# Row products moved behind the first gate groups, and another order for the first loads of a transformer block kernel

## The reference

```
h = rmsnorm(x) * g_attn;  p = h @ w_in            # 2048 x 4944, split into latents, q, k, v, indexer
y_a = latent attention (8 heads, low-rank q and kv, rotary, chunk mask)
y_b = sparse attention (8 heads, indexer picks 64 keys per query, relative bias)
x = x + concat(y_a, y_b) @ w_o
h = rmsnorm(x) * g_ffn
# PEER, per token and per head (8 heads):
score = (h @ w_pq) . sub_keys                     # 2 x 128 scores
top 16 of each half -> 256 sums -> top 16; expert = i0 * 128 + i1;  g = softmax(top sums)
x = x + sum_k g_k * gelu(u_tab[expert_k] . h) * v_tab[expert_k]     # tables 16384 x 2048
```

## Time and profile before

| | |
|---|---|
| time, median of 3 runs | 1678.68 us (1678.19 to 1679.05) |
| the profiled execution | 1682.57 us, its span 1680.8 us |
| TensorE busy | 1653.3 us (98%), granted clock 0.998 |
| VectorE, ScalarE, POOL busy | 1019.2, 503.3, 293.3 us |
| DMA | 569.90 MB, mean 339 GB/s |
| one u product on VectorE (L1136) | 2.29 us, the next starts 2.21 after it |
| one `gate` (L1198) | 1.17 us |
| one `hots` (L1184, two instructions) | 1.21 us from start to start of the next |
| one `apply` (L1208) | 0.32 us |
| a pair of u chunks with its gate group, from 790 to 1080 us | 9.48 us |

### The profile page before, as it was taken

The page is one execution under the profiler, slowest core; times in us unless marked ns, Lnnn a source line. Parts: engine busy times, 40 slices in busy tenths (PEclk is TensorE's granted clock), DMA queues, the critical chain, the costliest instruction groups (busy, mean ns, idle before and its releaser), DMA issues.

```text
span 1680.8 us, 28829 instructions
## 1 busy us (share of the span) xinstructions
PE 1653.3 (98%) x11428; PEld 1568.1 (93%) x11428; DVE 1019.2 (61%) x1708; ACT 503.3 (30%) x1346; POOL 293.3 (17%) x252
## 2 busy tenths in 40 slices
PE   7999999999999999989999999999999999999999
PEld 5768888888999999979999999999999999999998
DVE  5426695767778999767777667663334333433343
ACT  6547567656551000134454444420000000000000
POOL 1020000000003222322212111122212212223220
PEclk9999999999999999999999999999999999999999
DMA  9764445466648999999999999999999999999996
GB/s 337 240 142 131 138 132 194 138 223 204 224 154 347 421 403 421 397 400 421 394 422 406 421 408 422 375 388 416 417 415 417 417 416 422 422 422 422 421 417 236
DMA packets 107056, 569.90 MB, mean 339 GB/s; under 512 B 11280, under 2 KB 13456, under 8 KB 48208
## 3 DMA queue, kind: packets, MB, share of 16 engines
q1 hardware_dynamic: 57056, 216.51, 34.8%
q0 software_dynamic: 31792, 220.50, 32.7%
q10 hardware_dynamic: 18144, 132.13, 19.2%
HBM read 563.04 MB, written 4.46 MB: 338 GB/s over the span
## 4 chain that ended last, share of the span: by engine, by line
PE 78%; DVE 12%; DMA 6%; ACT 1%; issue 1%; POOL 1%; SPq 0%; DVEq 0%; ACTq 0%; POOLq 0%
PE ps L1574 32%; PE ps L1519 19%; PE ps L1315 5%; PE ps L1317 5%; PE ps L1316 5%; DVE late L1136 3%; PE ps L1334 2%; PE ps L1468 2%; PE ps L1536 2%; PE ps L1470 2%; PE ps L1469 2%; DMA raw<-in_w_in 1%; DMA acts<-in_u_rows,sel 1%; DMA late<-in_u_rows,sel 1%; DVE w_lo L817 1%
## 5 line engine op out<-in xcount | busy, mean ns | idle before, releaser
L1140 DVE SCALAR_TENSOR_TENSOR acts<-late,sel,acts 128x2048 f32<-128x2048 f32 x77 | 181.1, 2351 | 246.5 <-DMA late<-in_v_tab,sel 246.1
L1519 PE MATMUL ps<-acts,raw 128*128 128x160 f32 x2048 | 289.3, 301 | 0.0
L1519 PE MATMUL ps<-acts,late 128*128 128x160 f32 x2048 | 287.9, 300 | 0.0
L1574 PE MATMUL ps<-acts,late 128*128 (+1 forms) x2048 | 284.2, 299 | 0.0
L1574 PE MATMUL ps<-acts,raw 128*128 (+1 forms) x2048 | 283.6, 300 | 0.2 <-DMA raw<-in_v_tab 0.2
L1519 PEld LDWEIGHTS ps<-acts,raw 128*128 128x128 f32 x2048 | 282.1, 191 | 0.0
L1519 PEld LDWEIGHTS ps<-acts,late 128*128 128x128 f32 x2048 | 280.5, 190 | 0.0
L1574 PEld LDWEIGHTS ps<-acts,raw 128*128 128x128 f32 x2048 | 279.9, 190 | 0.6 <-issue 0.6
L1574 PEld LDWEIGHTS ps<-acts,late 128*128 128x128 f32 x2048 | 280.1, 190 | 0.1
L817 DVE TENSOR_TENSOR w_lo<-raw,w_hi 128x512 fp32r<-128x512 f32 (+1 forms) x288 | 188.8, 682 | 134.9 <-ACT w_hi L544 132.9
L1315 PE MATMUL ps<-w_hi,hT_hi 128*128 128x512 f32 (+1 forms) x448 | 185.7, 415 | 13.5 <-DVE w_lo L817 13.2
(11 more groups left out here) (220 smaller groups left out, 1575.7 us busy)
## 6 DMA issues: line engine op xcount, KB each, us to landing
raw<-in_w_in SPq DMA_DIRECT2D x72, 512.0 KB, 3.7
raw<-in_u_tab SPq DMA_DIRECT2D x33, 1024.0 KB, 9.7
late<-in_u_tab SPq DMA_DIRECT2D x33, 1024.0 KB, 9.9
raw<-in_v_tab SPq DMA_DIRECT2D x32, 1024.0 KB, 9.3
raw<-in_v_tab ACTq DMA_DIRECT2D x32, 1024.0 KB, 9.2
late<-in_v_tab SPq DMA_DIRECT2D x32, 1024.0 KB, 9.1
late<-in_v_tab ACTq DMA_DIRECT2D x32, 1024.0 KB, 9.3
raw<-in_u_tab ACTq DMA_DIRECT2D x31, 1024.0 KB, 9.7
```

What stands on the lines that cost most here:

```text
L1140: V.scalar_tensor_tensor(acc, row[n % NROW], w_sp[:, n - N_OWN:n - N_OWN + 1], acc, ALU.mult, ALU.add).then_inc(row_used, 1)
L1519: ins = mm(ps[:, q, 0:N_DN], ring[q][:, k * P:k * P + P], hF[:, k, :], start=k == 0, stop=k == KD - 1)
L1574: ins = mm(ps[:, pair_bank(k // 2), at:at + N_DN], ring[q][:, k * P:k * P + P], acts[:, ds(i * (4 * N_DN) + q * N_DN, N_DN)], start=first ...
```

## The change

It makes these edits.
- VectorE's order at the first gate groups: `next_row(4)` ahead of the slot transposes becomes `next_row(2)`, and three more products between `hots(1)` and `apply(FIRST_G + 1)` are taken away. To make up, the loop skips a product only where c % 16 is 15, and `WEIGH_AT` moves from 120 to 122.
- The first piece of xT and the gains are issued by ScalarE; SP begins with the first unit of w_in.
- POOL waits for the first half unit on TensorE before it issues iota, rope_tab, chunk_mask and rope_gain.
- ScalarE does an activation on a one-column tile first, TensorE does five matmuls on a zeroed tile first; VectorE sets both tiles and no longer waits for its memset.

```
-                if n == 0:
-                    sp.dma_start(gains[:, :], io["gains"]).then_inc(gain_in, 16)
+                if n:
+                    sp.dma_start(xT[:, k, :], io["xT"][:, k, :]).then_inc(xT_in[n], 16)
                 load(n, n, win[:, k, 0:512])
...
             pool.dma_start(acts[0:32, A_BIAS + 512:A_BIAS + 520], io["rel_bias"]).then_inc(hot_in, 16)
+            pool.wait_ge(piece_used, 1)
             pool.dma_start(iota[:, :], io["iota"]).then_inc(mask_in, 16)
...
+            act.dma_start(xT[:, 0:2, :], io["xT"][:, 0:2, :]).then_inc(xT_in[0], 16)
+            act.dma_start(gains[:, :], io["gains"]).then_inc(gain_in, 16)
+            act.wait_ge(warm_set, 1)
+            nc.scalar.activation(table_warm, carrier, ACT.Copy)
             act.wait_ge(gain_in, 16)
...
-            link(V.memset(kpad, 0.0))
+            V.memset(carrier, 0.0).then_inc(warm_set, 1)
+            V.memset(kpad, 0.0).then_inc(warm_set, 1)
...
-        WEIGH_AT = NKEY - 8
+        WEIGH_AT = NKEY - 6
...
             V.tensor_copy(w_sp, slot[:, 2, 0:N_PICK]).then_inc(gsp_ready, 1)
-            next_row(4)
+            next_row(2)
             dve.wait_ge(slotT_mm, TT)
...
             hots(0)
             hots(1)
-            next_row(2)
             apply(FIRST_G)
-            next_row()
             apply(FIRST_G + 1)
             next_row()
             gate(0)
             hots(2)
             apply(FIRST_G + 2)
             next_row()
             gate(1)
...
-                if rows_done[0] < N_OWN and c % 8 != 7:
+                if rows_done[0] < N_OWN and c % 16 != 15:
                     next_row()
...
+            pe.wait_ge(warm_set, 2)
+            for _ in range(5):
+                mm(ps[:, 6, 0:256], kpad[:, 0, :], early[:, 1024:1280], start=True, stop=True)
             for j in range(8):
                 pe.wait_ge(hTlo_done, 2 * j + 2)
```

More of the change, by code:

```diff
@@ L247, in build_block @@
         hs_in, idx_in, gsp_in, mask_set, acc_set, turn_kept = sem("hs_in"), sem("idx_in"), sem("gsp_in"), sem("mask_set"), sem("acc_set"), sem("turn_kept")
-        lent_in, acc_sum = sem("lent_in"), sem("acc_sum")
+        lent_in, acc_sum, warm_set = sem("lent_in"), sem("acc_sum"), sem("warm_set")
         gsp_ready, a_done, w_ready, acc_in = sem("gsp_ready"), sem("a_done"), sem("w_ready"), sem("acc_in")
@@ L365, in _ @@
                 k = slice(2 * n, 2 * n + 2)
-                sp.dma_start(xT[:, k, :], io["xT"][:, k, :]).then_inc(xT_in[n], 16)
-                if n == 0:
-                    sp.dma_start(gains[:, :], io["gains"]).then_inc(gain_in, 16)
+                if n:
+                    sp.dma_start(xT[:, k, :], io["xT"][:, k, :]).then_inc(xT_in[n], 16)
                 load(n, n, win[:, k, 0:512])
```

## The result

The changed kernel takes 1670.72 us (1668.14 to 1678.65, 20 runs), the kernel before on the same chips 1679.38 us (1675.95 to 1681.89, 20 runs). The ratio is 0.995, with a 95% interval of 0.9942 to 0.9957: 7.2 to 9.7 us less, by the medians 8.7. The forecast was 1667.3, 11.4 us less; the range, 1664.3 to 1672.3, holds the result, but it lies where the rival of the late rows was put, 1670 to 1675. The profiled execution of the changed kernel took 1671.05 us with a span of 1669.3.

The account below looks back on a forecast made before the run. TensorE was taken as the bound, busy 1653.3 of 1680.8 us. Gains of 10.9 us at the first gate groups and 0.5 at the head sum to 11.4: 1678.7 - 11.4 = 1667.3 us, range 1664.3 to 1672.3 for 8 in 10.

Parts of the forecast that it names:

- the rival of the late rows: Gathers fall behind and `hots` is late; TensorE waits 3 to 8 us between 800 and 1100 us: 1670 to 1675, chance 0.15.
- the hole: TensorE's two waits at gate groups 1 and 2, 740 to 760 us, plus slow matmuls behind: 10.97 us, taken as 10.9.
- The walk: Step through VectorE, ScalarE and TensorE at the first gate groups with measured durations: both waits close, 0.7, 0.7 and 0.2 us spare.
- the differences carry over: Gains read in the profiled execution, 1682.57 us, were taken to hold for the median of the runs, 1678.68, 3.9 lower.
- the moved products cost 0: Chunks 52 to 119 carry 64 products instead of 59; cost to TensorE taken as 0, bounds 0 to 8 us.
- the shortage: DMA in the later chunks: 429 GB/s wanted against 422 moved, 1.6% of 322 us, some 5 us spread over the stage.
- That buys nothing: Two of four products taken from ahead of the slot transposes gain nothing: VectorE already waited 1.36 us for the transposes.
- The head: Kernel start: TensorE begins at about 6.8 us; 2.6 us on paper, 0.5 us taken, bounds -0.7 and 2.6.
- its own sign: Unit 7 starting below 30 us would make the head worth its 2.6 us or more; about 31.4 was expected.
- The head in full: Rival: the waits at the gate groups close and the kernel's start pays 2.6 us: 1665.2, chance 0.17.
- One wait remaining: Rival: the second wait at the gate groups survives in part, gain 7.4 us: 1671.3, chance 0.08.
- the lend that breaks the cover: Rival: `lend_picks` makes rows 64 and 80 late, TensorE waits 8 us and pays 2.2 us of low clock: 1688, chance 0.03.

Follow-up runs that it names:

- The rows alone: The kernel before with only the moved row products, the new skips and the new `WEIGH_AT`: 1671.63 us, ratio 0.9946.
- constants early: The changed kernel without POOL's wait on the first half unit, so the four constants are issued at about 2.5 us: 1671.51 us, ratio 0.9953.
- loads later: The changed kernel with nine warm matmuls instead of five and the loads of x, w_uq and w_ukv released later: 1672.36 us, ratio 0.9951.
- picks early: The changed kernel with each copy of lent picks issued eight gathers ahead and waited for where it was: 1669.43 us, ratio 0.9937.
- old skips: The changed kernel with 7 products in 8 turns, as before the change, and `WEIGH_AT` at 126: 1670.28 us, ratio 0.9940.
- The head alone: The changed kernel with VectorE's order, the skips and `WEIGH_AT` of before: 1677.75 us, ratio 0.9986.
- second profile: The kernel before, unchanged, profiled once more: 1681.76 us in one run.
- last run: The changed kernel with gains ahead of x on ScalarE's queue, nine warm matmuls, later load releases and picks copied eight gathers ahead: 1670.63 us, ratio 0.9950.

## Why the prediction was right in sign and 3.4 us off in size

Of the 3.4 us, 0.7 is the kernel before, which took 1679.38 us over 20 runs and not 1678.68; 2.7 is the gain, 8.7 us instead of 11.4. The range held the result; the band of the forecast itself, 1666 to 1669.5, did not.

**Right: where the hole came from and that it closes.** The walk over VectorE, ScalarE and TensorE gave 5.0, 5.0 and 9.4 us between the gate groups; the trace shows 5.09, 5.07 and 9.47. The low clock left with the wait. The rows alone measure 9.1 us by the ratio.

**Wrong in size: "Gain 10.97 us; I take 10.9", with "the differences carry over".** The size was read from one execution, 3.9 us above the median, and a part of that excess lay in the hole itself: the row before the first wait of 2.88 us came late in that execution. Three profiles with the old order give 11.3, 8.4 and 9.3 us. With their mean the term is 9.7, 1.2 less. How much the median execution has is not known: the three profiles scatter by 2.9 us, and each is of an execution above its median.

**Wrong in size: the moved products cost 0.** The prediction has the shortage right (429 GB/s wanted, 422 carried) and calls it 5 us. But the two streams don't share it. A unit of u_tab per turn of 4.74 us is 1.049 MB / 4.74 = 221 GB/s and arrives on time; the rows get the rest, 420 - 221 = 199 GB/s, or 5.27 us a row. The queues of the changed kernel between 860 and 1080 us show it (q0 is POOL's, q1 and q10 are those of SP and ScalarE: packets, MB):

```profile
q0 software_dynamic: 6028, 43.42, 47.7%
q1 hardware_dynamic: 3312, 24.12, 26.7%
q10 hardware_dynamic: 3324, 24.22, 26.5%
```

That is 197 GB/s for the rows and 220 for the tables. The products of the changed kernel, once they wait, start 5.23 us apart (983.82 - 905.35 over 15 intervals of VectorE's timeline). The loop wants one each 4.74 x 16 / 15 = 5.06 us with the new skips and 4.74 x 8 / 7 = 5.42 with those of before. So 64 products fall short by up to 64 x 0.21 = 13 us less their lead, not by 5; and the skips of before fall short by nothing, as that run shows. TensorE felt little of it. Six profiles have the new pace and the picks copied late (changed, rows alone, no and nine warm matmuls, constants early, loads later): TensorE waits 0.2 to 2.1 us in 762 to 1108 us, mean 0.9, and from group 3 to the end they take 912.4 to 914.9 us, mean 913.5. The four with the picks early or the old skips take 911.9 to 913.4, mean 912.7, and the three with the old order 911.9, 914.0 and 911.9, mean 912.6. So the moved products give back some 0.9 us, between 0 and 2; the times of the three runs with picks early or old skips and nothing else changed, 1669.43 to 1670.28, are 0.4 to 1.3 us shorter, within their intervals.

The Trainium skill (DMA: Bandwidth & Descriptors, section Queues, rings and completion order) says that a DMA engine takes turns between the queues that have work. That agrees with a stream that wants less than its turn getting all of it and the other one the rest; the runs show the split, not the turns.

**Wrong: of the first two products, "That buys nothing".** It is true of the hole, since VectorE waited for the transposes in any case. It isn't true of the kernel: with them back it takes 4.9 us more. They were costed in VectorE's time, and they cost the rows' lead. Without this part the change would have met the rival of the late rows: 4.2 us of waits on TensorE in 762 to 1108 us, 1675.57 us.

**The head.** That TensorE calls in the loads it then waits for is confirmed by the two runs with nine warm matmuls, and it goes on up to unit 17. But with the new head and its slow start there was no such waiting up to 32 us in any of the seven profiles with five warm matmuls. Unit 7 starts at 28.5 to 30.2 us in them, in four of them below 30, against 31.88, 31.23 and 29.84 with the old head, where the prediction had 31.4. By its own sign the term of 0.5 was too small in the traces. Its steps are off: TensorE was put at 6.8 us and starts at 8.02, because the gains, 21 KB issued behind x, land 4.5 us after issue; and the warming, put at 1.2 to 1.4 us, spares nothing (ten slow matmuls without it, six to thirteen with it); 2.15 us of idling follow it. Group 0 comes at 738.0, 738.0 and 736.2 with the old head and at 735.0 to 736.5, mean 735.6, in the seven profiles with the new one and its five warm matmuls: 1.8 us, where the prediction took 0.5. The head alone measures 2.4 us (0.8 to 3.9), and on top of the rows nothing that stands out (1671.63 to 1670.72). Between 0 and 2 us is what can be said. The constants are not needed for it: with them early, group 0 still comes at 736.3. The earlier unit and x are what is left; they were not tried singly, so the cause stays open.

**The sum again.** 9.7 for the hole, 0 to 2 for the head, 0 to 2 given back: 7.7 to 11.7, about 9.8 in the middle (9.7 + 1 - 0.9), and the measured interval is 7.2 to 9.7. The middle is 1 us too high; a hole of 8.4 us, as in the second profile, would give 8.5. The runs don't decide which term the rest belongs to.

**The rivals.** The late rows happened, but nearly all under TensorE's cover: it waited 1.13 us, where that rival had 3 to 8. The time lies in that rival's band mostly because the hole had been read too large, so the band fits by luck. The head in full (1665.2) fell: nothing that starts the head earlier keeps it. One wait remaining, and the lend that breaks the cover, did not come, although the picks alone now took 22.4 us, where the prediction had 24 for picks and first row.

**Two slips that don't enter the forecast.** The prediction puts the time lost to the low clock at 1.4 us, but its own rows give 0.62 + 1.62 = 2.24 in the hole alone. And with 2.2 us of low clock at each of two places, a late `lend_picks` would eat the gain from 11.4 / 2 - 2.2 + 7 = 10.5 us of lateness, not from 12.7.

## What to carry to other kernels

- A wait read from one profile is a sample. If that execution is longer than the median, the excess may be in the very wait that the change removes; read the wait in a second profile before it is taken at full length.
- When two streams share full DMA engines and one of them is paced, the other carries the whole shortage. Take the missing bandwidth as a share of the stream that gives way, not of the sum: 1.6% of all bytes was 3 to 4% of the rows.
- Work moved under an engine's idle time is free only for that engine. Ask what it draws from the queues, and when.
- A head that is bound by bytes can't be started earlier into a gain: look for the last unit that waits on a load, not the first.

## What the hardware showed that was not expected

- Warming that stops 2.1 to 3.0 us ahead of the work was worth nothing: 6 to 13 slow matmuls with it, 10 without. In the run with the picks early the warming itself had sped up, 4.16 us for what takes 4.63, and the first real matmul still took 0.55 us, neither 0.47 nor 0.77; the granted clock was 0.60 at 8 to 9 us and 0.50, the 1.2 GHz level, at 9 to 11. So it had risen in the warming and fell when the real work had begun. Warming that ended 1.1 to 1.4 us ahead left none of the first 84 matmuls slow, in three kernels.
- A wait in the midst of work can cost clock behind it, and how much isn't a matter of its length alone. The run with nine warm matmuls waited 2.35 us ahead of unit 7, then ran six matmuls at full speed and six at the low level; the last run waited 2.35 us ahead of unit 18 and none was slow; a wait of 2.88 us cost nothing either.
- A slower start can end sooner. With six and seven slow matmuls the old head then waited 2.2 and 2.1 us for weights; the same head with 12 of them did not wait and reached unit 8 at 33.60 instead of 35.75 and 35.08. The new head did not wait with six slow matmuls (unit 8 at 32.26), but did with none (36.49).
- A copy of 2 KB from partition to partition takes 16.8 us behind gathers in the kernel before, 22.4 in the changed one and 11.4 with the skips of before: the more gathers are under way, the longer it takes. That it waits for their bytes is a reading of these three numbers and was not tried by itself.
